# The sums of squares of a norm move from ahead of the second up block into its middle, in a two-model transformer kernel on one core

## The reference, cut to what matters

```
def rms_norm_2(x, g, eps=1e-6):
    xf = x.astype(jnp.float32)
    y = xf * lax.rsqrt(jnp.mean(xf * xf, axis=-1, keepdims=True) + eps)
    return (y * g.astype(jnp.float32)).astype(x.dtype)

def swiglu_2(x, w_in, w_out):
    gate, up = jnp.split(x @ w_in, 2, axis=-1)
    return (jax.nn.silu(gate) * up) @ w_out

for i in range(DEPTH):
    h = x + 0.5 * swiglu_2(rms_norm_2(x, norm_ffn1[i]), w_ffn1_in[i], w_ffn1_out[i])
    u = rms_norm_2(h, norm_mix[i])
    ...
    h = h + 0.5 * swiglu_2(rms_norm_2(h, norm_ffn2[i]), w_ffn2_in[i], w_ffn2_out[i])
    x = h + (p[i] @ w_pe_proj[i]) * jax.nn.sigmoid(rms_norm_2(h, norm_pe[i]) @ w_pe_gate[i])
```

## Time and profile before

| what | us |
| --- | --- |
| median of 3 runs | 2393.3 (2392.12 to 2394.8) |
| profiled execution, span | 2386.1 |
| PE busy | 2276.9 (95%) |
| DVE busy | 1649.5 (69%) |
| ACT busy | 1177.1 (49%) |
| POOL busy | 183.2 (8%) |
| mean granted clock of TensorE | 0.989 of 2.4 GHz |

### The profile page before, as it was taken

One profiled execution on the slowest core, in us unless ns is written; L12 is line 12 of the kernel. 1 busy time (PEld: TensorE's weight loads), 2 busy tenths in 40 slices (PEclk: granted clock), 3 DMA queues, 4 the chain that ended last, 5 costly groups with the idle time before them and its releaser, 6 DMA issues.

```text
span 2386.1 us, 40670 instructions
## 1 busy us (share of the span) xinstructions
PE 2276.9 (95%) x16788; PEld 2148.3 (90%) x16788; DVE 1649.5 (69%) x1725; ACT 1177.1 (49%) x1198; POOL 183.2 (8%) x185
## 2 busy tenths in 40 slices
PE   4999889999989998999899999999999999999999
PEld 4997888799789877899799998999999999899999
DVE  5996786786589876855655569865465546996555
ACT  2443555455355445454455454655355536465534
POOL 0110000010001100000012000012001200001200
PEclk9999999999999999999999999999999999999999
DMA  8996433586568752554554543445454544345453
GB/s 346 352 353 228 159 135 124 203 317 248 194 237 353 309 197 88 192 197 176 175 186 177 186 153 120 145 180 187 176 181 160 186 183 159 106 159 177 176 185 137
DMA packets 75936, 471.53 MB, mean 198 GB/s; under 512 B 8707, under 2 KB 8963, under 8 KB 27580
## 3 DMA queue, kind: packets, MB, share of 16 engines
q1 hardware_dynamic: 53136, 383.80, 43.8%
q0 software_dynamic: 18976, 68.71, 7.7%
q10 hardware_dynamic: 3724, 17.56, 2.0%
HBM read 468.97 MB, written 1.06 MB: 197 GB/s over the span
## 4 chain that ended last, share of the span: by engine, by line
PE 77%; DVE 11%; ACT 5%; DMA 4%; issue 2%; ACTq 0%; DVEq 0%; SPq 0%
PE ab L1769 48%; PE acc L1769 13%; PE acc L1891 10%; DVE wlo L966 3%; DMA modmem<-mods 2%; ACT whi L419 2%; PE mb L2120 1%; DMA raw<-stream 1%; DMA par<-params 1%; PE mb L1942 1%; DVE sc L1051 1%; DVE sc L1580 1%; PE acc L2148 1%; PE mb L1769 0%; PE mb L2009 0%
## 5 line engine op out<-in xcount | busy, mean ns | idle before, releaser
L1769 PE MATMUL ab<-u_hi,whi 128*128 128x256 f32 x3664 | 1052.1, 287 | 26.7 <-DVE u_lo L1148 10.7
L1769 PE MATMUL ab<-u_lo,whi 128*128 128x256 f32 x3664 | 1043.0, 285 | 0.0
L1769 PE MATMUL ab<-u_hi,wlo 128*128 128x256 f32 x3664 | 1042.5, 285 | 0.0
L966 DVE TENSOR_TENSOR wlo<-raw,whi 128x2048 fp32r<-128x2048 f32 x361 | 824.8, 2287 | 311.8 <-ACT whi L419 309.9
L419 ACT ACTIVATE whi<-raw 128x2048 fp32r<-128x2048 f32 x361 | 688.9, 1910 | 535.9 <-DMA raw<-stream 338.4
L1769 PEld LDWEIGHTS ab<-u_hi,whi 128*128 128x128 f32 x3664 | 709.8, 194 | 42.0 <-issue 31.5
L1769 PEld LDWEIGHTS ab<-u_lo,whi 128*128 128x128 f32 x3664 | 709.9, 194 | 0.4
L1769 PEld LDWEIGHTS ab<-u_hi,wlo 128*128 128x128 f32 x3664 | 709.5, 194 | 0.0
L1769 PE MATMUL acc<-h_hi,whi 128*128 128x256 f32 (+1 forms) x1032 | 294.0, 285 | 4.8 <-DVE h_lo L1517 2.6
L1769 PE MATMUL acc<-h_lo,whi 128*128 128x256 f32 (+1 forms) x1032 | 292.7, 284 | 0.0
L1769 PE MATMUL acc<-h_hi,wlo 128*128 128x256 f32 (+1 forms) x1032 | 292.5, 283 | 0.0
(11 more groups left out here) (323 smaller groups left out, 1995.5 us busy)
## 6 DMA issues: line engine op xcount, KB each, us to landing
raw<-stream SPq DMA_DIRECT2D x365, 1024.0 KB, 4.8
modmem<-mods POOLq DMA_DIRECT2D x128, 512.0 KB, 6.3
sc<-lnrows ACTq DMA_DIRECT2D x5, 1024.0 KB, 4.7
sc<-start ACTq DMA_DIRECT2D x4, 1024.0 KB, 16.5
gateb<-gaterows ACTq DMA_DIRECT2D x6, 512.0 KB, 3.9
hank<-toep POOLq DMA_DIRECT2D x8, 192.0 KB, 4.1
x<-xT ACTq DMA_DIRECT2D x1, 1024.0 KB, 31.3
x<-xn ACTq DMA_DIRECT2D x1, 1024.0 KB, 4.9
```

Source lines behind the costliest of these rows:

```text
L966: nc.vector.tensor_tensor(wlo[:, n % RAW, :], raw[:, n % RAW, :], whi[:, n % RAW, :].bitcast(F32), ALU.subtract).then_inc(lo_ready, 1)
L1769: ins = nc.tensor.matmul(out, l, r, start=first and i == 0, stop=last and i == 2, skip_group_check=True)
```

## The change

`a_block` and `a_static` get an argument `between`, a function called between the two halves of an up block. `ffn_a` hands its new argument `within` to the second up block. For the first FFN of each layer of the second model `squares` is now given as `within` and no longer as `behind`: TensorE waits for the sums and makes the two products after the first 24 matmuls of the second up block, not ahead of them. The second FFN of each layer keeps its order, and so do `window` and `extra`.

```diff
-            def a_block(n, an, it=None, ms=(0, 1)):
+            def a_block(n, an, it=None, ms=(0, 1), between=None):
...
                 for m in ms:
+                    if between is not None and m == 1:
+                        between()
                     for k in range(DM):
...
-            def a_static(n=1, ms=(0, 1)):
+            def a_static(n=1, ms=(0, 1), between=None):
                 for _ in range(n):
-                    a_block(g[0], a[0], None, ms)
+                    a_block(g[0], a[0], None, ms, between)
...
-            def ffn_a(behind=None):
+            def ffn_a(behind=None, within=None):
                 first_block()
                 if behind is not None:
                     behind()
-                a_static(1)
+                a_static(1, between=within)
...
-            def ffn2(behind):
-                ffn_a(behind)
+            def ffn2(behind, within):
+                ffn_a(behind, within)
...
             for l in range(DEPTH):
-                ffn2(squares)
+                ffn2(None, squares)
                 window(l)
-                ffn2(squares)
+                ffn2(squares, None)
                 extra(l)
```

## The result

The changed kernel took 2398.97 us (median of 20 runs, 2390.75 to 2404.2) against 2391.74 us (20 runs, 2386.94 to 2396.5). The ratio is 1.0029, 95% interval 1.0022 to 1.0036, or +7 us; timed again it was 1.0030 (1.0018 to 1.0042). The forecast was 2395.3 us, +2.0 us, with a range up to 2398.4. The direction was right, the size was not: the loss is over three times the sum.

What follows compares the result with a forecast made beforehand. TensorE (77% of the chain) was taken as the bound, with block 3's wlo late next. Layer 0 -0.33 + 1.3 and layer 1 -0.28 + 1.3 gave +2.0 us on 2393.3: 2395.3 us, range 2391.4 to 2398.4.

Steps and rivals of the forecast that it cites:

- The chain that the prediction followed: First FFN of each layer: products, root, block 3's whi and wlo splits, block 3; root to wlo's end 6.02 us.
- the price of the clock: Low clock stretch behind the new idle at block 3: 1.3 us per layer, bounds 0 and 3.16 us.
- Layer 1's root: Norm's square root on ACT in layer 1: starts at 1795.27, now 1794.99, 0.28 us later.
- The products run 0.83 us later than now, but at the high clock: Layer 0, after block 2's first half: products at 1193.94 against 1193.11, without a long idle in front.
- What hides it is the first half: Layer 0: block 2's first half, 2.88 us, covers the moved wait for the sums, which then costs nothing.
- The gains of 0.33 and 0.28 us: Block 3 starts earlier, at 1201.09 in layer 0 (0.33 us) and 1801.36 in layer 1 (0.28 us).
- a part that may pass while TensorE is still idle: Idle ahead of block 3: part of the low stretch passes there, so 1.3 us is taken, not 1.58.
- The sum that the prediction gave for that case: Both layers: each new idle ahead of block 3 ends in a clock fall at full price, +2.55 us.
- (A): Rival: block 3 isn't bound by the norm's end, so the wait just goes; -7.4 us, 2385.9; chance 0.04.
- (B): Rival: block 3 waits, but the clock stays high through both new gaps; -0.6 us, 2392.7; chance 0.12.
- (D): Rival: moved products still find TensorE waiting, block 2's first half late by as much; no change, 2393.3; chance 0.02.
- (C): Rival: from block 3, two low clock stretches in a row in both layers; +5.7 us, 2399.0; chance 0.07.

Runs made afterwards that it cites:

- mid_early: Changed kernel with block 3's two weight splits put ahead of the norm's square root (ACT) and reciprocal (DVE): 2386.12 us, ratio 0.9978.
- after_k6: Changed kernel with the two products after 18 matmuls of block 2 in place of 24: 2395.17 us, ratio 1.0010.
- after_end: Changed kernel with the two products behind all 48 matmuls of block 2, in both layers: 2403.99 us, ratio 1.0059.
- mid_fill: Changed kernel with 26 further matmuls, result unread, behind the second up block in the idle ahead of block 3: 2393.18 us, ratio 0.9996.
- before_look1: The kernel before, unchanged, profiled once more: 2386.19 us, one run.
- change_look3: The changed kernel as it is, a third profiled execution: 2400.74 us, one run.
- l1_only: The change in layer 1 alone, layer 0 as in the kernel before: ratio 0.9998.
- l1_only_again: The change in layer 1 alone, timed and profiled a second time: ratio 1.0006.
- l0_only_again: The change in layer 0 alone, layer 1 as in the kernel before, timed and profiled a second time: ratio 1.0013.
- front_fill: The kernel before with 18 further matmuls, result unread, in its 2.2 us idle between block 1 and the products: 2393.21 us, ratio 1.0001.
- after: The changed kernel, both layers, in its first profiled execution; timed at 2398.97 us, ratio 1.0029.
- change_again: The changed kernel as it is, timed and profiled once more: ratio 1.0030.

## Why the prediction missed, and what of it was right

The forecast was +2.0 us, the loss is +7 us, above the whole range. The chain that the prediction followed is the right one. What it had wrong is when block 1 ends, the root's gain, the price of the clock, and two terms left out: the spread of its reference and the attention parts.

- **The mechanism was right in its first step.** Block 3's wlo took the place of the wait. Idle of 3.33 and 3.34 us was measured where 3.25 and 3.26 us was forecast, released by L966, and a low stretch behind it in both layers. mid_early, after_k6 and after_end show that this chain sets when block 3 starts, mid_fill that the low stretch costs 1.5 us in each layer.
- **Layer 1's root was right.** From the start of the last sum to the reciprocal, 3.24 us was measured; the steps of the prediction give 0.70 for the rest of the sum, 1.95 to the root and 0.50 to the reciprocal, 3.15 us.
- **"The products run 0.83 us later than now, but at the high clock" failed in layer 0.** This is the step that failed most. They did run at the high clock, but the prediction let block 1 end when it had ended in the one execution it read. There block 1 was fast. In all three profiled executions of the changed kernel it was slow, and its end, not wlo, released block 2. This costs 4.97 - 3.15 = 1.8 us. "What hides it is the first half" was true of the sums' wait; but the 2.2 us of idle were themselves the cover for a slow block 1, and the prediction counted them as waste alone.
- **The gains of 0.33 and 0.28 us aren't gains against a typical execution.** The root was forecast 0.20 us earlier (layer 0) and 0.28 us later (layer 1) than in a profile whose products ran at the low clock, in part or in full. In before_look1 they didn't: the root starts 1.22 us behind the sums in both layers and the norm's stretch is 17.8 us. The changed kernel's root comes 2.05 us behind them in layer 1, so the move makes it 0.8 us later. With this the account closes: block 3 takes 7.34 us behind its idle and 5.85 us in before_look1, where it waits 0.45 us for wlo and no low stretch follows, so 17.8 + 0.8 + 1.5 = 20.1 us, where layer 1 has 20.1 to 20.2 us in two of the three executions; with 1.7 us for the slow block 1 it is 21.8 us, where layer 0 has 21.9 us.
- **The price of the clock was too low, and its source was misread.** 1.3 us was taken, 7.34 - 5.78 = 1.56 us was paid in each layer of this execution, and 8.48 - 5.78 = 2.7 us once (change_look3, layer 1). The 1.58 us that the prediction worked out from block 1 of layer 1 is near this by luck. That block takes 7.22 us in before_look1 too, at the full clock, because it waits twice for a quarter of u (start us, us, instruction, idle before; then the stretch over the block, with its granted clock of 1.00):

```profile
1784.89 0.38 PE L1769 MATMUL ab<-u_hi,whi 128*128 128x256 f32 x1 [0.57 <-DVE u_lo L1244]
1787.01 0.39 PE L1769 MATMUL ab<-u_hi,whi 128*128 128x256 f32 x1 [0.43 <-DVE u_lo L1244]
1782.60:1790.13 7.53, 6.48 (x48) 5.92 (x48) 7.15 (x11) 6.30 (x12) 0.00 (x0) 1.00 0.30 122
```

- **The discount for "a part that may pass while TensorE is still idle" had no row behind it.** In the changed kernel's profile both stretches began 1 us or more after block 3 had started. In four of the ten places listed at the end a stretch did begin inside the idle, by 0.3 to 1.1 us; the two single ones of these (l1_only, l1_only_again) still cost 1.4 us. The Trainium skill ("TensorE: Matmul & The Clock Gate", section "What's actually happening") has the low level as the default that activity releases. All ten places agree with it: each idle of 3.3 us has a low stretch in it or behind it. The sum that the prediction gave for that case, +2.55 us, was nearer than the forecast, and still short for the reasons of the other points.
- **The reference was one execution.** Its stretches of 18.8 and 18.7 us contain products and a block 2 at the low clock. The mean of five is 18.0 and 18.2 us. That is 0.7 us in layer 0 and 0.5 us in layer 1 by which the kernel before had more to lose than its first profile says. Against that first profile, layer 0 comes out as 0.97 forecast + 1.8 + 0.26 of clock = 3.0 us, where 21.9 - 18.8 = 3.1 us was measured.
- **The attention parts were left out of the sum.** They follow the norm's stretch: from that L1022 to the DVE instruction of L1580 that starts at 1501.50 (layer 0) and at 2102.09 us (layer 1) in the kernel before. This took 294.0 + 294.4, 295.9 + 294.4 and 294.8 + 296.5 us in the three executions of the kernel before (mean 590.0), and 296.0 + 295.1 us in all three of the changed one (591.1). The 1.1 us go with the low stretches: TensorE's wait for ACT's L700 there is 1.3 us where a low stretch ended some 15 us ahead of it, and 2.4 us where none did. With the 5.6 us of the norms this makes 6.7 us of the 7.2. That the change causes this last part is argued, not shown: unchanged layers show both values too. The whole second model agrees with the timing: from the wlo split that starts layer 0's stretch to the end of the profiled span it takes 1197.4, 1197.8 and 1200.1 us before, and 1205.3, 1205.2 and 1208.2 us after, 7.8 us more in the mean. So the loss as timed lies in the second model.
- **Rivals.** (A) is out, (B) is out: the clock fell behind all of the new idle stretches. (D) is out. (C) gave about the right time for another reason; among the three executions of the changed kernel the second low stretch in a row came once, in one layer (l0_only_again has it too). The rival that was missing is the buffer: a late block 1 that the products now wait for.

What stays open: block 1 of layer 0 was slow in three of three executions of the changed kernel, for the whole of its run up to 1196.2 in the first, and in one of three of the kernel before (and in l1_only). It was as slow (8.3 us from its first to its last matmul) in mid_fill, front_fill and after_end, and faster (6.15 to 7.4 us) in the other nine. The low stretch starts at 1186, ahead of anything that the change moves, so chance is the plain reading, but the runs can't exclude an effect of the code's place.

## What to carry to other kernels

Before a wait is filled with work, ask what else stood in its shadow: here the next block's split hung on the product that was moved back, and a slow block ahead of it had been absorbed by the idle. Move the work that is next in line first (block 3's split ahead of the square root), then the wait can be filled: the same move cost 7 us without it and gained 4 to 7 us with it. And read several executions of the kernel before: a price that depends on the granted clock differs by 1 us from one to the next, in the kernel that one subtracts from too.

## What the runs showed of the hardware

- An idle of TensorE of 3.3 us brought a low stretch of the clock in all ten places where it was profiled with the change as it is (after, change_again and change_look3 twice each, the four runs of a single layer once each). In six of them it began 0.7 to 1.4 us after the work had resumed, in four of them inside the idle. A single low stretch that begins behind the idle, inside dense matmuls, makes the step from block 3 to block 4 7.34 us long, against 5.85 us behind a short wait at the full clock (mid_fill, before_look1): 1.5 us.
- 26 matmuls that nobody reads, in place of 3.1 us of idle, made the kernel 6 us faster by the medians and 3.0 us by the norm's stretches. Filling the old idle of 2.2 us, which also serves as a buffer (front_fill), won nothing.
- Identical code spreads by some 10 us from run to run (2386.9 to 2396.5 us in 20 runs of the kernel before), and the granted clock varies with it: the profiled executions of the kernel before took 2386.1, 2384.4 and 2390.4 us at a mean clock of 0.989, 0.994 and 0.986.
